# Norm, turn and router of the first layer norm done one token tile at a time, in a kernel of two transformer blocks

## The chip, the cores and the metric

The program runs on one core of one Trainium2 chip. The metric is the device time in microseconds (us) of one execution. Before the change three executions took 1676.92 to 1677.72 us, median 1677.66 us.

## The reference

The input x has 256 tokens of 1024 numbers (two tiles of 128 tokens, t = 0 and 1). It passes through a first block of two layers (retention and stick-breaking attention, then SwiGLU), and then through a second block of two layers, l = 0 and 1. All is float32. One layer of the second block, cut to what matters here:

```python
mix = hybrid_mixer(x, ...)                       # three kinds of attention, then a product with w_o
x = layer_norm(ALPHA * x + mix, ln1_g, ln1_b)    # "the first norm"
# hier_moe:
lg = x @ rg_w + rg_b                             # 4 groups; the best group per token
le = x @ re_w + re_b                             # 8 experts a group; the best two of that group
y = sum over experts of gate * (silu(x @ w_gate) * (x @ w_up)) @ w_down
x = layer_norm(ALPHA * x + y, ln2_g, ln2_b)
```

## The kernel before

The program is written engine by engine, each with its own instruction stream, and semaphores join them. An engine executes strictly in the order of its stream. A helper `Signal` numbers the increments of a semaphore by layer, so that `x.at(l, k)` is the k-th increment in layer l.

**Products.** Dense weights are 1 MB units that SyncE's queue loads into a ring of six slots. ScalarE (ACT, L917 and L933) writes the rounded high half of a unit, VectorE (DVE, L924 and L939) the low half, and TensorE (PE) does three products of halves for each full one (L946, L947, L950).

**Dummies.** `keep_running(acc, n)` (L1256) issues n matmuls of 512 columns on ones whose result nobody reads. They are there so that TensorE is not idle.

**The stretch that is changed, once per layer of the second block.** `output_unit(3)` finishes the four quarters `wo` of the attention output (two halves of columns for each token tile). VectorE adds each to H (L2887) and takes its moments (L2877, L2898, L2899). GpSimd (POOL) takes the power -1/2 (L3239), one number per token. VectorE then computes `shift` for tile 0 (L2892). ScalarE writes the normed tile 0, Z[:, 0] (L2262), and VectorE tile 1 (L2902). Both read H with a stride of 8 elements and write Z in blocks, so that each block of 128 columns holds every eighth column of H. TensorE, after 16 dummies, turns (transposes) the sixteen 128x128 blocks (`turn_z`, L1580); a bank `xT2` holds two values of k for both tiles. ScalarE and VectorE take four k each out of the banks to T8, with gain and bias of the norm (L2268, L2906). The router (L1788) multiplies T8 with 36 columns: eight k times two tiles, in the order in which the k come. Next to that ScalarE writes H_high, the rounded high half of Z (L2259), and VectorE H_low, the rest (L2882), in both tiles with the low half of tile 1 placed after `chosen` and ahead of `rank`.

**From the router to the experts.** VectorE runs a chain of small operations on the logits (L2916 to L2942, ending in `chosen_done`). TensorE meanwhile issues 8 and 4 dummies, and then counts ranks (L1799 to L1803). VectorE makes rank (L2962) and the first one-hot picks (L2953, `make_picks(0, 0)`), then goes on to the gate weights (L2965 to L2988, `gate_done`), with two small exponentials on ScalarE in between. TensorE gathers the tokens of the first two pairs of experts ("duos") by matmuls with the picks (`gather(0, f)`, L1819): for each of four banks, two k, and for each k high and low half of both tiles, 32 in all. It waits for both low halves before. `turn_picks(0)` (L1833) waits for `gate_done`. ScalarE (L2284) and VectorE (L3002) take the gathered banks to XG; `gate_up2(0)` (L1860) starts the experts.

**The experts.** Sixteen duos follow one another on TensorE; per duo the weights are 6 MB. SyncE's queue issues a load when the slot it goes to is released by TensorE. One slot of duo 0 lies in T8, and is loaded once the router is filled.

**The seam between the blocks.** After the last product of the first block TensorE issues 26 dummies, then `turn_stream` turns both tiles of H (L1568). For layer 1 five dummies lie between its tiles, for layer 0 none. Tile t is ready after `last_norm(t)` (VectorE, L2630). ScalarE splits three weight units (L933) and then the turned stream (L2160), from which the first projection is fed.

Of the kernel before, what the change touches and what calls it, by code (L numbers as in the profile page):

```python
# [345 lines left out]
def build(nc, src, out, debug=None):  # L346
# [7 lines left out]
    with ctx:  # L354
# [311 lines left out]
        head_var = signal("head_var", HR)  # L666
# [29 lines left out]
        xT2_act = signal("xT2_act", 4)  # L696
# [51 lines left out]
        split_high = signal("split_high", TT)  # L748
# [18 lines left out]
        def in_blocks(view):  # L767
            return view.rearrange("p (k n) -> p k n", k=KT)

# [36 lines left out]
        for kp in range(4):  # L806
            read2["xT", kp] = (bT_low, kp + 5)
            read2["xT2", kp] = ((xT2_act, xT2_dve)[kp % 2], 2 * (kp // 2) + 2)
# [426 lines left out]
        def _(pe):  # L1235
# [324 lines left out]
            def turn_stream(l):  # L1560

                for t in range(TT):
# [8 lines left out]
                    if t == 0 and l > 0:  # L1571
                        keep_running(bank2(("A", 1)), 5)

            def turn_z(l):

                for t, done in enumerate((z_act, z_dve)):
                    pe.wait_ge(done.sem, done.at(l, 1))
                    for k in range(KT):
                        acc = claim2(("xT2", k // 2), l) if t == 0 and k % 2 == 0 else bank2(("xT2", k // 2))
                        mm = nc.tensor.transpose(acc[:, k % 2 * SEQ + t * P:k % 2 * SEQ + (t + 1) * P],  # L1580
                                                 Z[:, t, k * P:(k + 1) * P], ident[:])
                        if t == TT - 1 and k % 2 == 1:
                            fill(mm, ("xT2", k // 2))
# [120 lines left out]
            keep_running(bank_of(("gu", 2 * PAIRS - 1)), 26)  # L1704
            for l in range(LAYERS):
# [75 lines left out]
                keep_running(bank2(("xT2", 3)), 16)  # L1781
                turn_z(l)
                acc = bank2(("router", 0))
                for n, k in enumerate((0, 2, 1, 3, 4, 6, 5, 7)):
                    signal_ = (xT2_act, xT2_dve)[k // 2 % 2]
                    pe.wait_ge(signal_.sem, signal_.at(l, k // 4 * 2 + k % 2 + 1))
                    for t in range(TT):
                        mm = nc.tensor.matmul(acc[:, t * 64:t * 64 + 36], T8[:, k, t * P:(t + 1) * P], rw[:, k, :],  # L1788
                                              start=(n == 0 and t == 0), stop=(n == KT - 1 and t == TT - 1))
# [15 lines left out]
                def moe_pass(pass_):  # L1805
# [5 lines left out]
                    def gather(g, n):  # L1811
# [4 lines left out]
                        for j, k in enumerate((2 * n, 2 * n + 1) if group_parts(g) == 4 else (n,)):  # L1816
                            for n_ in range(2 * TT):
                                t, part = divmod(n_, 2)
# [5 lines left out]
                                                      start=(n_ == 0), stop=(n_ == 2 * TT - 1))  # L1824
                        fill_p(mm, "xg", g, n)
# [157 lines left out]
        def _(act):  # L1983
# [179 lines left out]
            for l in range(LAYERS):  # L2163
# [93 lines left out]
                def high_of_z(t):  # L2257

                    nc.scalar.activation(moe_split(H_high[:, t, :]), Z[:, t, :], ACT.Copy).then_inc(split_high.sem, 1)  # L2259
# [1013 lines left out]
```

## Time and profile before

| what | us |
|---|---|
| three executions, median | 1677.66 |
| the profiled execution, its own time | 1679.14 |
| its span, first to last instruction | 1677.4 |
| TensorE busy | 1645.6 (98%) |
| VectorE busy | 856.5 (51%) |
| ScalarE busy | 651.1 (39%) |
| GpSimd busy | 172.1 (10%) |

The mean granted clock of TensorE is 0.995 of full speed. Busy TensorE counts dummies too, so 98% does not say that the engine does useful work all the time. In the second block of layer 0 the stretch of the change is at 1007 to 1030 us of the span, in layer 1 at 1415 to 1438 us. The seam between the blocks is at 855 to 863 us. The rows below give start, duration and what ended the idle time before.

### The profile page before, as it was taken

How to read it: one execution, taken by the hardware profiler on the slowest of the kernel's cores; microseconds unless marked ns; L12 is line 12 of the kernel's file. 1: busy time of each engine (PE TensorE's matmuls, PEld its weight loads, DVE VectorE, ACT ScalarE, POOL GpSimd, SP SyncE). 2: the span in 40 equal slices, each digit the busy share in tenths (PEclk: the TensorE clock that was granted, in tenths of full speed). 3: DMA queues.
4: the chain of work that ended last, by engine and by line, in shares of the span. 5: the costliest groups of instructions: out<-in, count | busy, mean ns of one | idle time of the engine just before them, and what ended most of it. 6: DMA issues, size and time to landing. Idle time of an engine off the chain costs nothing. (4 is left out here: it accounts for less than half of the span.)

```text
span 1677.4 us, 23534 instructions
## 1 busy us (share of the span) xinstructions
PE 1645.6 (98%) x9403; PEld 1244.0 (74%) x9403; DVE 856.5 (51%) x1420; ACT 651.1 (39%) x920; POOL 172.1 (10%) x242
## 2 busy tenths in 40 slices
PE   9999999999999999999999999999999999999997
PEld 7888879999798887999988975444448887544442
DVE  6566564444646556544456867322126785532223
ACT  5455444343445454434345453111114464211111
POOL 2020001111202000111111040000002023000000
PEclk9999999999999999999999999999999999999999
DMA  8544545553654455455356546999995636699996
GB/s 319 180 146 147 179 151 183 194 178 123 235 184 134 151 176 176 167 185 188 137 185 194 189 142 231 408 421 421 421 397 191 192 127 241 228 421 420 421 417 259
DMA packets 158587, 396.61 MB, mean 236 GB/s; under 512 B 20752, under 2 KB 85264, under 8 KB 140048
## 3 DMA queue, kind: packets, MB, share of 16 engines
q1 hardware_dynamic: 158480, 395.18, 64.6%
q8 instruction: 67, 1.10, 0.3%
q14 instruction: 40, 0.33, 0.1%
HBM read 394.10 MB, written 1.05 MB: 236 GB/s over the span
## 5 line engine op out<-in xcount | busy, mean ns | idle before, releaser
L946 PE MATMUL ps<-split,split 128*128 128x256 f32 (+3 forms) x1872 | 631.6, 337 | 1.2 <-DVE split L939 0.7
L950 PE MATMUL ps<-split,split 128*128 128x256 f32 (+3 forms) x1872 | 627.6, 335 | 0.1
L947 PE MATMUL ps<-split,split 128*128 128x256 f32 (+3 forms) x1872 | 623.6, 333 | 0.0
L924 DVE TENSOR_TENSOR split<-ring,split 128x2048 fp32r<-128x2048 f32 x136 | 312.5, 2305 | 253.9 <-ACT split L917 253.8
L946 PEld LDWEIGHTS ps<-split,split 128*128 128x128 f32 x1872 | 351.6, 188 | 36.1 <-issue 2.1
L950 PEld LDWEIGHTS ps<-split,split 128*128 128x128 f32 x1872 | 351.7, 188 | 35.8 <-DVE split L2389 1.2
L947 PEld LDWEIGHTS ps<-split,split 128*128 128x128 f32 x1872 | 352.9, 189 | 33.0 <-issue 0.5
L917 ACT ACTIVATE split<-ring 128x2048 fp32r<-128x2048 f32 x136 | 260.3, 1916 | 278.1 <-PE ps L950 268.7
L1860 PE MATMUL ps<-ring,arena 128*64 128x512 f32 x464 | 105.7, 592 | 0.0
L3040 DVE SCALAR_TENSOR_TENSOR arena<-arena,ps 128x256 f32<-128x256 f32 x32 | 15.4, 480 | 169.8 <-ACT arena L2306 134.1
L1860 PE MATMUL ps<-arena 128*64 128x512 f32 x288 | 99.5, 594 | 0.5 <-SPq L1208 0.5
L939 DVE TENSOR_TENSOR split<-ring,split 128x1536 fp32r<-128x1536 f32 (+3 forms) x44 | 80.8, 1852 | 25.2 <-ACT split L933 25.0
L1860 PE MATMUL ps<-high,arena 128*64 128x512 f32 x256 | 92.0, 592 | 1.6 <-DMA arena<-in_expert_w_up 1.6
L3052 DVE TENSOR_TENSOR split<-ps,split 128x512 fp32r<-128x512 f32 x64 | 44.3, 692 | 92.2 <-ACT split L2313 92.2
L2306 ACT ACTIVATE arena<-ps 128x256 f32<-128x256 f32 x32 | 12.3, 384 | 202.9 <-PE ps L1860 202.9
L933 ACT ACTIVATE split<-ring 128x1536 fp32r<-128x1536 f32 (+3 forms) x44 | 67.7, 1547 | 49.2 <-PE ps L950 48.4
L1860 PEld LDWEIGHTS ps<-ring,arena 128*64 128x64 f32 x464 | 34.3, 137 | 64.0 <-issue 63.9
L2313 ACT ACTIVATE split<-ps 128x512 fp32r<-128x512 f32 x64 | 38.2, 597 | 107.1 <-PE ps L1886 107.1
L1860 PEld LDWEIGHTS ps<-high,arena 128*64 128x64 f32 x256 | 29.1, 137 | 60.2 <-issue 60.2
L1900 PE MATMUL ps<-split,split 128*128 128x512 f32 x240 | 64.2, 402 | 0.0
L1819 PEld LDWEIGHTS ps<-split,split 128*128 128x128 f32 x320 | 43.9, 190 | 25.2 <-issue 25.2
L1886 PE MATMUL ps<-ring,arena 128*64 128x512 f32 x256 | 58.5, 598 | 0.1
(260 smaller groups left out, 1698.8 us busy)
## 6 DMA issues: line engine op xcount, KB each, us to landing
ring<-in_w_in SPq DMA_DIRECT2D x52, 1024.0 KB, 5.1
ring<-in_w_gate_up SPq DMA_DIRECT2D x44, 1024.0 KB, 5.3
ring<-in_expert_w_down SPq DMA_DIRECT2D x32, 1024.0 KB, 13.0
ring<-in_w_down SPq DMA_DIRECT2D x22, 1024.0 KB, 4.9
ring<-in_w_in SPq DMA_DIRECT2D x28, 768.0 KB, 4.5
ring<-in_expert_w_gate SPq DMA_DIRECT2D x20, 1024.0 KB, 11.8
ring<-in_expert_w_up SPq DMA_DIRECT2D x20, 1024.0 KB, 13.8
arena<-in_expert_w_down SPq DMA_DIRECT2D x16, 1024.0 KB, 14.5
```

The source lines that it names most:

```text
L917: nc.scalar.activation(split(high[:, n % HIGH, :]), ring[:, units[key], :], ACT.Copy).then_inc(high_done.sem, 1)
L924: nc.vector.tensor_tensor(split(slot), slot, split(high[:, n % HIGH, :]), ALU.subtract).then_inc(low_done.sem, 1)
L933: nc.scalar.activation(split(high[:, n % HIGH, 0:used(key)]), ring[:, units2[key], 0:used(key)], ACT.Copy).then_inc(high2_done.sem, 1)
L939: nc.vector.tensor_tensor(split(slot), slot, split(high[:, n % HIGH, 0:used(split2[n])]), ALU.subtract).then_inc(low2_done.sem, 1)
L946: nc.tensor.matmul(acc, sh, mh, start=start, stop=False)
L947: nc.tensor.matmul(acc, *second, start=False, stop=False)
L950: return nc.tensor.matmul(acc, *third, start=False, stop=stop)
L1819: mm = nc.tensor.matmul(acc[:, j * SEQ:j * SEQ + XG_cols[g]].rearrange("p (e n) -> p e n", n=TAKEN_SLOTS), moe_split((H_high, H_low)[part] ...
L1860: mm = nc.tensor.matmul(acc[i * SLOTS:(i + 1) * SLOTS, :].rearrange("p (s n) -> p s n", s=2), XG[g % 2][:, at:at + SLOTS], w_[:, :, k % w_ ...
L1886: mm = nc.tensor.matmul(bank2(("yg", 0, d, half))[i * SLOTS:(i + 1) * SLOTS, :], hT[:, d % 2, j * P + i * SLOTS:j * P + (i + 1) * SLOTS], ...
L1900: mm = nc.tensor.matmul(bank2(("sc", 0, i)), moe_split(pickT[:, d % 2, (TT - 1 - t) * P:(TT - t) * P]), moe_split(Y[:, part, half * 512:(h ...
L3052: nc.vector.tensor_tensor(moe_split(Y[:, 1, cols]), acc, moe_split(Y[:, 0, cols]), ALU.subtract).then_inc(y_low.sem, 1)
```

## The change

Tile 0 and tile 1 are handled one after the other. Z is written in the columns' own order; whoever needs blocks reads it with a stride. The 16 dummies before the turns become 6, the 26 at the seam become 10, and five more stand between the tiles of the stream in layer 0 as well. ScalarE takes all eight k of tile 0 and four of tile 1 to T8, VectorE four of tile 1, in instructions of half the size. The high half of tile 0 is made by GpSimd, that of tile 1 by ScalarE at the end; both low halves remain on VectorE, that of tile 0 ahead of the logits, that of tile 1 after the first picks. `shift` moves to GpSimd. The first gather does the high halves of all four banks first and then the low halves.

```diff
-            keep_running(bank_of(("gu", 2 * PAIRS - 1)), 26)
+            keep_running(bank_of(("gu", 2 * PAIRS - 1)), 10)
...
-                    if t == 0 and l > 0:
+                    if t == 0:
                         keep_running(bank2(("A", 1)), 5)
...
+            def turn_z(t, l):
+                done = (z_act, z_dve)[t]
+                pe.wait_ge(done.sem, done.at(l, 1))
+                for k in range(KT):
+                    key = ("xT2", 2 * t + k // 4)
+                    acc = claim2(key, l) if k % 4 == 0 else bank2(key)
+                    mm = nc.tensor.transpose(acc[:, k % 4 * P:(k % 4 + 1) * P], Z[:, t, k::KT], ident[:])
+                    if k % 4 == 3:
+                        fill(mm, key)
+            def route(t, l):
+                acc = bank2(("router", 0))
+                ks = range(KT) if t == 0 else (0, 4, 1, 5, 2, 6, 3, 7)
+                for n, k in enumerate(ks):
...
+                    mm = nc.tensor.matmul(acc[:, t * 64:t * 64 + 36], T8[:, k, t * P:(t + 1) * P], rw[:, k, :],
+                                          start=(n == 0 and t == 0), stop=(n == KT - 1 and t == TT - 1))
...
-                keep_running(bank2(("xT2", 3)), 16)
-                turn_z(l)
...
+                keep_running(bank2(("xT2", 3)), 6)
+                turn_z(0, l)
+                route(0, l)
+                turn_z(1, l)
+                mm = route(1, l)
                 fill(mm, ("router", 0))
...
-                        pe.wait_ge(split_low.sem, split_low.at(l, TT))
+                        pe.wait_ge(split_high.sem, split_high.at(l, 1))
+                        pe.wait_ge(high1_in.sem, high1_in.at(l, 1))
...
-                    for f in range(group_parts(0)):
-                        gather(0, f)
+                    for part in range(2):
+                        if first and part == 1:
+                            pe.wait_ge(split_low.sem, split_low.at(l, TT))
+                        for f in range(group_parts(0)):
+                            gather(0, f, part)
... ScalarE
-                nc.scalar.activation(in_blocks(Z[:, 0, :]), H[:, 0, :].rearrange("p (n k) -> p k n", k=KT), ACT.Identity,
-                                     scale=rstd2[:, 0:1], bias=shift[:, 0:1]).then_inc(z_act.sem, 1)
-                act.wait_ge(z_act.sem, z_act.at(l, 1))
-                high_of_z(0)
-                for k in (0, 1, 4, 5):
+                nc.scalar.activation(Z[:, 0, :], H[:, 0, :], ACT.Identity, scale=rstd2[:, 0:1],
+                                     bias=shift[:, 0:1]).then_inc(z_act.sem, 1)
+                for t, k in [(0, k) for k in range(KT)] + [(1, k) for k in range(4, KT)]:
...
                 act.wait_ge(z_dve.sem, z_dve.at(l, 1))
-                high_of_z(1)
+                nc.scalar.activation(moe_split(in_blocks(H_high[:, 1, :])), of_blocks(Z[:, 1, :]),
+                                     ACT.Copy).then_inc(high1_in.sem, 1)
... VectorE
-                    if i == 3:
-                        dve.wait_ge(rstd_done.sem, rstd_done.at(l, 1))
-                        nc.vector.scalar_tensor_tensor(out=shift, in0=mv2[:, 0, 0:1], scalar=-1.0, in1=rstd2[:, 0:1], ...)
...
-                nc.vector.tensor_scalar(in_blocks(Z[:, 1, :]), H[:, 1, :].rearrange("p (n k) -> p k n", k=KT), ...)
-                for k in (2, 3, 6, 7):
+                nc.vector.tensor_scalar(Z[:, 1, :], H[:, 1, :], mv2[:, 1, 0:1], rstd2[:, 1:2], ALU.subtract, ALU.mult)
+                for k in range(4):
...
-                low_of_z(0)
+                dve.wait_ge(split_high.sem, split_high.at(l, 1))
+                nc.vector.tensor_tensor(moe_split(in_blocks(H_low[:, 0, :])), of_blocks(Z[:, 0, :]), ...)
...
-                low_of_z(1)
                 dve.wait_ge(chosen_done.sem, chosen_done.at(l, 1))
...
                 make_picks(0, 0)
+                dve.wait_ge(high1_in.sem, high1_in.at(l, 1))
+                nc.vector.tensor_tensor(moe_split(in_blocks(H_low[:, 1, :])), of_blocks(Z[:, 1, :]), ...)
... in the expert loop, duos 1 and 3: the same product of Z and gain, now without rearranging
-                                out=H[:, d // 2, :].rearrange("p (n k) -> p n k", k=KT),
-                                in0=Z[:, d // 2, :].rearrange("p (k n) -> p n k", k=KT), scalar=ALPHA,
+                                out=H[:, d // 2, :], in0=Z[:, d // 2, :], scalar=ALPHA, in1=lng[:, 0, :], op0=ALU.mult,
... GpSimd, after the power of tile 0
+                        nc.gpsimd.tensor_scalar(shift, mv2[:, 0, 0:1], rstd2[:, 0:1], -1.0, ALU.mult,
+                                                ALU.mult).then_inc(shift_in.sem, 1)
+                wait_apart(pool, z_act.sem, z_act.at(l, 1))
+                wait_apart(pool, z_dve.sem, z_dve.at(l, 1))
+                nc.gpsimd.tensor_copy(moe_split(in_blocks(H_high[:, 0, :])),
+                                      of_blocks(Z[:, 0, :])).then_inc(split_high.sem, 1)
```

## Rows read from the trace of the kernel before

**Rows 1.** Timeline of TensorE, layer 0 (start us, us, engine line operation count)

```profile
1011.26 3.63 PE L1259 MATMUL ps<-ones 128*128 128x512 bf16 x16
1014.82 1.97 PE L1580 MATMUL ps<-ident,arena 128*128 128x128 f32 x16
1016.79 3.76 PE L1788 MATMUL ps<-arena,T 128*128 128x36 f32 x32
1020.38 2.76 PE L1259 MATMUL ps<-ones 128*128 128x512 bf16 x12
...
1025.85 3.77 PE L1819 MATMUL ps<-split,split 128*128 128x160 f32 x32 [0.99 <-DVE split L2953]
1029.46 0.40 PE L1833 MATMUL ps<-split 128*128 128x192 f32 x2
```

**Rows 2.** Timeline of ScalarE, layer 0

```profile
1012.53 2.24 ACT L2262 ACTIVATE arena<-H,arena 128x1024 f32<-128x1024 f32 x1 [9.25 <-DVE arena L2892]
...
1016.17 1.93 ACT L2268 ACTIVATE T<-ps,arena 128x256 f32<-128x256 f32 x4 [0.30 <-PE ps L1580]
...
1028.77 0.86 ACT L2284 ACTIVATE arena<-ps,arena 128x160 f32<-128x160 f32 x2 [0.93 <-PE ps L1819]
```

**Rows 3.** Timeline of VectorE, layer 0

```profile
1016.39 1.90 DVE L2906 TENSOR_SCALAR T<-ps,arena 128x256 f32<-128x256 f32 x4 [0.79 <-PE ps L1580]
...
1020.66 0.23 DVE L2916 TENSOR_TENSOR arena<-ps,arena 128x72 f32<-128x72 f32 x1 [1.10 <-PE ps L1788]
...
1023.55 1.22 DVE L2882 TENSOR_TENSOR split<-arena,split 128x1024 fp32r<-128x1024 f32 x1
1024.69 0.22 DVE L2962 SCALAR_TENSOR_TENSOR arena<-ps,arena 128x64 f32<-128x64 f32 x1
1024.94 0.76 DVE L2953 SCALAR_TENSOR_TENSOR split<-arena 128x256 fp32r<-128x256 f32 x2
...
1028.13 0.23 DVE L2988 TENSOR_TENSOR split<-arena,split 128x64 fp32r<-128x64 f32 x1
1028.28 0.79 DVE L3002 TENSOR_SCALAR arena<-ps,arena 128x160 f32<-128x160 f32 x2
```

**Rows 4.** Timeline of GpSimd, layer 0

```profile
1010.70 0.57 POOL L3239 TENSOR_TENSOR arena<-arena,minus_half 128x1 f32<-128x1 f32 x1 [21.75 <-DVE arena L2899]
```

**Rows 5.** Groups by line and shape, whole span (count, busy us, mean ns, idle before)

```profile
L2341 ACT ACTIVATE arena<-H,arena 128x1024 f32<-128x1024 f32 x4 | 4.6, 1150 | 5.7 <-DVE arena L3083 5.7
L3174 POOL CAST split<-arena 128x256 fp32r<-128x256 f32 x44 | 17.5, 397 | 305.3 <-DVE arena L2604 303.9 <-issue 1.4
L3243 POOL TENSOR_SCALAR arena<-arena 128x1 f32<-128x1 f32 x4 | 0.8, 190 | 490.2 <-ACT arena L2341 490.0
```

**Rows 6.** Timeline of TensorE, layer 1, the same stretch

```profile
1424.54 4.29 PE L1788 MATMUL ps<-arena,T 128*128 128x36 f32 x32
1428.63 3.93 PE L1259 MATMUL ps<-ones 128*128 128x512 bf16 x12
```

**Rows 7.** Stretches: span, busy us (count) of PE, PEld, DVE, ACT, POOL; granted clock, DMA share, GB/s

```profile
1428.00:1429.00 1.00, 1.00 (x5) 0.77 (x6) 0.07 (x1) 0.00 (x0) 0.00 (x0) 0.50 1.06 438
1028.00:1036.00 8.00, 8.00 (x47) 3.89 (x48) 7.29 (x25) 2.14 (x3) 0.00 (x0) 1.00 0.03 10
1048.00:1250.00 202.00, 200.82 (x968) 92.76 (x965) 47.92 (x102) 35.12 (x70) 0.00 (x0) 1.00 1.01 416
```

**Rows 8.** Timelines at the seam between the blocks: TensorE, ScalarE, VectorE

```profile
855.08 5.79 PE L1259 MATMUL ps<-ones 128*128 128x512 bf16 x26
860.70 1.96 PE L1568 MATMUL ps<-ident,H 128*128 128x128 f32 x16
...
859.72 1.59 ACT L933 ACTIVATE split<-ring 128x1664 fp32r<-128x1664 f32 x1 [0.83 <-DMA ring<-in_w_in]
862.01 2.38 ACT L2160 ACTIVATE split<-ps 128x256 fp32r<-128x256 f32 x8 [0.70 <-PE ps L1568]
...
858.02 1.28 DVE L2630 SCALAR_TENSOR_TENSOR H<-H,stat,arena 128x1024 f32<-128x1024 f32 x1 [0.66 <-POOL stat L3137]
```

More of the change, by code:

```diff
@@ L665, in build @@
         gates = signal("gates", 4)
-        head_var = signal("head_var", HR)
+        head_var = signal("head_var_then_high1", HR)
         head_rstd = signal("head_rstd", HR)
@@ L695, in build @@
         bT_low = signal("bT_low", 16)
-        xT2_act = signal("xT2_act", 4)
+        xT2_act = signal("xT2_act", 12)
         xT2_dve = signal("xT2_dve", 4)
@@ L746, in build @@
         resid_in = signal("resid_in", 2 * TT)
-        split_high = signal("split_high", TT)
+        split_high = signal("split_high", 1)
+        high1_in = Signal(head_var.sem, 1, LAYERS * HR)
         split_low = signal("split_low", TT)
@@ L768, in in_blocks, with of_blocks @@
             return view.rearrange("p (k n) -> p k n", k=KT)
+        def of_blocks(view):
+            return view.rearrange("p (n k) -> p k n", k=KT)
         def bank_of(key):
@@ L1570, in turn_stream @@
                             fill(mm, ("xT", b))
-                    if t == 0 and l > 0:
+                    if t == 0:
                         keep_running(bank2(("A", 1)), 5)
[L1574 to L1583, printed above, removed]
+            def turn_z(t, l):
[11 more added lines that the diff above has]
+                for n, k in enumerate(ks):
+                    if t == 0:
+                        pe.wait_ge(xT2_act.sem, xT2_act.at(l, k + 1))
+                    elif k < 4:
+                        pe.wait_ge(xT2_dve.sem, xT2_dve.at(l, k + 1))
+                    else:
+                        pe.wait_ge(xT2_act.sem, xT2_act.at(l, 8 + k - 3))
+                    mm = nc.tensor.matmul(acc[:, t * 64:t * 64 + 36], T8[:, k, t * P:(t + 1) * P], rw[:, k, :],
+                                          start=(n == 0 and t == 0), stop=(n == KT - 1 and t == TT - 1))
+                return mm
             def index_scores(h, l):
@@ L1780, in _ @@
                 output_unit(3, l)
-                keep_running(bank2(("xT2", 3)), 16)
-                turn_z(l)
[L1783 to L1789, printed above, removed]
+                keep_running(bank2(("xT2", 3)), 6)
[3 more added lines that the diff above has]
+                mm = route(1, l)
                 fill(mm, ("router", 0))
@@ L1809, in fill_p, with gather @@
                         mm.then_inc(filled[banks2[(name, 0) + key]], 1)
-                    def gather(g, n):
+                    def gather(g, n, only=None):
                         lo, hi = GROUP_DUOS[g]
@@ L1817, in gather @@
                             for n_ in range(2 * TT):
-                                t, part = divmod(n_, 2)
+                                part, t = divmod(n_, TT)
+                                if only not in (None, part):
+                                    continue
                                 mm = nc.tensor.matmul(acc[:, j * SEQ:j * SEQ + XG_cols[g]].rearrange(
@@ L1823, in gather @@
                                                           "p (e n) -> p e n", n=SLOTS)[:, :, 0:TAKEN_SLOTS]),
-                                                      start=(n_ == 0), stop=(n_ == 2 * TT - 1))
-                        fill_p(mm, "xg", g, n)
+                                                      start=(n_ == 0 and (j == 0 or only is None)),
+                                                      stop=(n_ == 2 * TT - 1 and (only is None or j == 1)))
+                        if only != 0:
+                            fill_p(mm, "xg", g, n)
                     def turn_picks(d):
@@ L2889, in _ @@
                                                    op1=ALU.add).then_inc(wo_in.sem, 1)
-                    if i == 3:
-                        dve.wait_ge(rstd_done.sem, rstd_done.at(l, 1))
-                        nc.vector.scalar_tensor_tensor(out=shift, in0=mv2[:, 0, 0:1], scalar=-1.0, in1=rstd2[:, 0:1],
-                                                       op0=ALU.mult, op1=ALU.mult).then_inc(shift_in.sem, 1)
                     dve.wait_ge(wo_in.sem, wo_in.at(l, i + 1))
@@ L2964, in _ @@
                 make_picks(0, 0)
+                dve.wait_ge(high1_in.sem, high1_in.at(l, 1))
+                nc.vector.tensor_tensor(moe_split(in_blocks(H_low[:, 1, :])), of_blocks(Z[:, 1, :]),
+                                        moe_split(in_blocks(H_high[:, 1, :])), ALU.subtract).then_inc(split_low.sem, 1)
                 nc.vector.tensor_tensor(shifted, logit[:, :, 0:GROUPS],
```

25 lines of the change are left out of this document (11 added, 14 removed).

## The prediction

> **What bounds the kernel now.** I read the view of stretches first, for the places where something other than the products ends the wait. Expert weights fill the DMA engines from 1048 to 1250 us (share 1.01), but from 1028 to 1036 us they stand nearly still (0.03) [rows 7]. So the stream of weights has no backlog when the experts begin, and its later loads go out as TensorE releases slots: what TensorE gains ahead of the experts moves the stream too, and comes out at the end. Then the timelines of the engines over the stretch of the norm. TensorE looks busy, but from 1011.26 to 1014.8 and again from 1020.38 it is busy with dummies [rows 1]; the work is a chain over engines. ScalarE waits 9.25 us for `shift` and then needs 2.24 us for Z [rows 2]; the turns start 0.05 us behind its end, at 1014.82; the router's passes run one behind another for 3.76 us, each pair a matmul of float32 in two passes, so 3.76 / 32 = 0.118 us a pass, twice that a product [rows 1]. VectorE starts on the logits at 1020.66, and at 1023.55, right behind the chain's end, it puts 1.22 us of low half in front of rank, which starts at 1024.69 [rows 3]. The gather starts at 1025.85, `turn_picks` at 1029.46 [rows 1], and the experts 0.3 us later. All this is on the path, twice in the program. At the seam of the blocks the turns stand behind 26 dummies until 860.70, while tile 1 was ready at 858.02 + 1.28 = 859.30 [rows 8].
>
> **The seam.** A dummy takes 3.63 / 16, less the tail of the last, about 0.22 us [rows 1]. Ten end at 855.08 + 2.2 = 857.3, the turns of tile 0 (half of 1.96) at 858.2, five dummies at 859.3, the turns of tile 1 at about 860.3, 2.2 us before now. ScalarE is the next to be late: its third weight unit ends at 859.72 + 1.59 = 861.31, bound by that unit's landing, which the change does not touch. So L2160 starts at 861.3 instead of 862.01 [rows 8], and **0.7 us** of the 2.2 remain. Bounds: 0 (if VectorE's low halves of the next unit are what counts) and 2.2.
>
> **Z of tile 0.** The power ends at 1010.70 + 0.57 = 1011.27 [rows 4]; a POOL operation on one number takes 0.19 us [rows 5], with the hand-over some 0.4, so `shift` is there at 1011.7 instead of about 1012.5. The stride goes from the read: the nearest row without one is 1.15 us [rows 5] instead of 2.24. Z is ready at 1012.85 instead of 1014.77. Six dummies end at 1011.26 + 1.3 = 1012.6, so they do not hold it. Tile 1's Z on VectorE is not late even at today's speed, since today all turns are done at 1016.8.
>
> **Turns and router.** Eight turns take half of 1.97. The first bank is full 0.6 us after the start, 1013.45. ScalarE takes now eight small pieces: four of 256 columns take 1.93 us, two of 160 take 0.86 [rows 2], so 0.46 and 0.4 us a piece; I take 0.36 for 128 columns (bounds 0.25, half the row of 256 with its pipeline, and 0.46). Eight end at 1013.5 + 8 x 0.36 = 1016.4. TensorE's router for tile 0 goes at their pace and ends 0.4 later; being in order, the turns of tile 1 are behind it: 1016.85 to 1017.8. Then VectorE's four pieces from 1017.5 (1.90 us for 256 columns today [rows 3], 1.3 to 1.4 for 128) to 1018.9, ScalarE's four from 1017.95 to 1019.45, and the last product ends at about 1020.0. Router for router: 1020.5 now, so 0.5 us. At 0.25 us a piece it would be 1.8 us, at 0.46 a loss of 0.7.
>
> **Halves.** VectorE has the low half of tile 0 behind its pieces: 1018.9 + 1.22 = 1020.1. It is as late as the router, so logits start at 1020.2 instead of 1020.66: **0.45 us**. The low half waits for GpSimd's copy. A cast of 256 columns takes 0.397 us [rows 5], 1024 some 1.5 us; it starts behind both Z, at 1015.6 at the latest, and has until 1018.9. No row shows GpSimd reading with this stride; ScalarE with it needed 2.24 for 1.15, and twice 1.5 still ends at 1018.6. It costs nothing up to 3.3 us. The Trainium skill (GPSIMD Engine Reference, Performance pitfalls for Q7 kernels) gives +50% for reads with a step over 8 bytes; by that it would end near 1017.9, an estimate from that page. ScalarE's high half of tile 1, at most 2.24 us from 1019.5, is there before 1022. The 1.22 us between `chosen` and rank go: the ranks' matmuls take some 0.4 us in their place, so rank starts 0.45 + 0.65 = **1.1 us** earlier, and so does the gather: 1024.75.
>
> **Gather.** Its 16 high products (1.9 us) cover the low half of tile 1, which now follows the picks on VectorE and ends at 1025.8. Hidden; without that cover it would cost 1.0 us. But VectorE's chain to `gate_done` begins behind it. That chain takes from 1025.70 to 1028.36 now [rows 3]; behind 1025.7 it ends at 1028.4, no earlier. TensorE ends its gather at 1024.75 + 3.6 = 1028.35. `turn_picks` starts at 1028.45 instead of 1029.46: **1.0 us** for layer 0. The banks now fill only in the second half of the gather, but still 0.47 us apart; ScalarE has its first at 1028.2 and VectorE at 1029.1, before `gate_up2` asks at 1028.8 and 1029.6. The slot in T8 is asked for only at its second half, 3.5 us on, when the weights, still from 1028 on, have landed. The straight product in duos 1 and 3 shortens VectorE under TensorE's cover: nothing.
>
> **The clock.** In layer 1 the granted clock was 0.50 from 1428 to 1429 us, the lower level of 1.2 GHz [rows 7], after the turns and most of the router. In layer 0 the same router products kept their pace of 2.4 GHz. The router took 4.29 instead of 3.76 us, the twelve dummies 3.93 instead of 2.76 [rows 1, 6]. Without a fall after the change, layer 1 gains 1.0 and these 0.5: **1.5 us**. But the change takes ten full dummies away, and spreads the same thin products over 7.4 us (1012.6 to 1020.0), with gaps, where it was 5.6. I expect the fall more often. Its price: at the least the 0.53 of the router and, of the dummies' 1.17 us, what exceeds their slack (they end 0.65 us before `chosen`), 0.5: 1.05 us. At the most the tile 1 turns and all router products of tile 1 run at half rate: turns 0.9 longer, the products 16 x 0.118 = 1.9 longer less what waits on ScalarE anyhow: 2.5 us. I take 1.8. The Trainium skill (TensorE: Matmul & The Clock Gate, Avoid-throughput-drops row of Why this matters for your kernels) warns of gaps between bursts of matmuls, which speaks against this change; this trace agrees as far as that the clock fell behind thin work, while the engine was busy throughout.
>
> **The sum.** Without a fall 0.7 + 1.0 + 1.5 = 3.2 us less; the profiled execution of 1679.14 (span 1677.4, 1.7 around it) would be 1675.9. It was 1.5 above the median of the runs, 1677.66, which would be 1674.5. With one fall 1.8 goes: 1676.3.
>
> **Rivals.** *No fall:* 1674.5. For it: layer 0 had none. Chance 0.25. *Deep falls in both layers*, the case on the other side: 2.5 us in each, so 3.2 - 5.0, 1.8 us slower, 1679.5. It decides from 1.6 us a layer on. For it: the thinner sequence and the fall in layer 1. Against it: the late fall there cost only 0.5 us. Chance 0.2. *The weights hide it:* if the stream from 1048 on is the bound whatever TensorE does before, only the seam counts: 1677.0. Against it the still DMA from 1028 to 1036. Chance 0.05. *Smaller pieces cost as much as large ones:* 0.46 us a piece, 12 on ScalarE in a row, takes 1.2 a layer away from my 1.0 and 1.5: 1674.5 + 2.4 = 1676.9 without a fall, 1679.0 with two at the least price. Chance 0.1.
>
> **Numbers.** The forecast, one fall of middle price or two cheap ones, has 0.4: 1676.3 us, its own range 1675 to 1677.7. From the cheap end of the pieces without a fall to deep falls it is 1673.6 to 1679.7, which I give as range. 0.2% is 3.4 us, about what a measurement here can tell from no change: faster than 1674.3 takes the case without a fall and pieces a little cheaper than mine, or a fall in layer 1 before that is usual and now gone: 0.29. Slower than 1681.0 takes deep falls and dear pieces: 0.06. The rest, 0.65, is within.
>
> **What would show it.** After: Z of tile 0 at 1.1 to 1.2 us in ScalarE's rows, turns right behind; pieces of 128 columns at 0.36 us; logits about 0.45 us earlier after the last w_o product than now and rank 0.4 us behind `chosen`; gather without idle between its halves; granted clock of 0.5 in at least one layer between turns and ranks; L2160 0.7 us earlier at the seam. I would be wrong if VectorE waits for GpSimd at the low half of tile 0, if idle time stands before `gate_up2(0)`, or if TensorE's idle time behind the weights (DMA) grows by what the front gained.

## The result, and the profile after

The changed kernel takes 1682.7 us, the median of 8 executions (1681.63 to 1683.89), the kernel before in the same session 1677.69 us (8 executions, 1676.71 to 1678.17). The ratio is 1.003, 95% interval 1.0021 to 1.0039: slower by 5.0 us. The forecast was 1676.3 us, with a range up to 1679.7. The profiled execution took 1681.64 us, its span 1679.9. Of all executions below, one, at 3856.43 us (e10), is a disturbed one and counts in no ratio.

The first view is TensorE's timeline in layer 0, with ScalarE, VectorE and GpSimd behind it (start us, us, engine line operation, count, idle time and its releaser).

```profile
1010.61 1.47 PE L1263 MATMUL ps<-ones 128*128 128x512 bf16 x6
1012.41 1.16 PE L1585 MATMUL ps<-ident,arena 128*128 128x128 f32 x8 [0.33 <-ACT arena L2281]
...
1016.36 1.12 PE L1585 MATMUL ps<-ident,arena 128*128 128x128 f32 x8
1017.54 2.24 PE L1600 MATMUL ps<-arena,T 128*128 128x36 f32 x16
...
1025.14 3.97 PE L1836 MATMUL ps<-split,split 128*128 128x160 f32 x32 [0.40 <-DVE split L2963]
1029.75 0.47 PE L1852 MATMUL ps<-split 128*128 128x192 f32 x2 [0.64 <-DVE split L3001]
...
1011.12 1.24 ACT L2281 ACTIVATE arena<-H,arena 128x1024 f32<-128x1024 f32 x1 [8.48 <-POOL arena L3254]
1013.16 2.90 ACT L2285 ACTIVATE T<-ps,arena 128x128 f32<-128x128 f32 x8 [0.81 <-PE ps L1585]
...
1018.90 2.08 ACT L2289 ACTIVATE split<-arena 128x1024 fp32r<-128x1024 f32 x1
...
1017.08 1.36 DVE L2915 TENSOR_SCALAR T<-ps,arena 128x128 f32<-128x128 f32 x4 [2.56 <-PE ps L1585]
1018.36 2.01 DVE L2918 TENSOR_TENSOR split<-arena,split 128x1024 fp32r<-128x1024 f32 x1
...
1020.53 0.23 DVE L2927 TENSOR_TENSOR arena<-ps,arena 128x72 f32<-128x72 f32 x1
...
1024.91 2.13 DVE L2976 TENSOR_TENSOR split<-arena,split 128x1024 fp32r<-128x1024 f32 x1
...
1029.47 0.23 DVE L3001 TENSOR_TENSOR split<-arena,split 128x64 fp32r<-128x64 f32 x1
...
1014.69 2.03 POOL L3258 CAST split<-arena 128x1024 fp32r<-128x1024 f32 x1 [1.02 <-DVE arena L2911]
```

The starts of two profiles differ by what happened long before, so times are counted here from the end of the last product of w_o, where the first dummies begin (1011.26 before [rows 1], 1010.61 after). Turns start at 1.80 (3.56 before), and the last router product ends at 9.17 (9.29). But the logits start on VectorE at 9.92, later than before (9.40), with no idle time in front: the engine had only just ended its low half (L2918), which takes 2.01 us now that it reads Z with a stride, where L2882 took 1.22 [rows 3]. (Its other two operands, the high half that it reads and the low half that it writes, lie in blocks and are gone through straight, before and after: one operand of three has the stride.) The second low half (L2976) takes 2.13, pushes the gate weights (L3001) back, and the gather takes 3.97 us where it took 3.77 [rows 1]; `turn_picks` (L1852) then stands idle 0.64 us for the gate weights. Before there was no idle time there [rows 1]; it started at 18.20, now at 19.14.

In layer 1 more is lost. TensorE's timeline, and then the view of stretches (span, busy us and count of PE, PEld, DVE, ACT, POOL, granted clock, DMA share, GB/s):

```profile
1421.05 3.06 PE L1600 MATMUL ps<-arena,T 128*128 128x36 f32 x16
1423.91 1.95 PE L1585 MATMUL ps<-ident,arena 128*128 128x128 f32 x8
...
1426.41 3.20 PE L1600 MATMUL ps<-arena,T 128*128 128x36 f32 x14 [0.26 <-ACT T L2285]
1429.42 4.92 PE L1263 MATMUL ps<-ones 128*128 128x512 bf16 x12
...
1440.36 0.47 PE L1852 MATMUL ps<-split 128*128 128x192 f32 x2 [0.65 <-DVE split L3001]
```

```profile
1422.00:1423.00 1.00, 1.00 (x8) 0.84 (x7) 0.00 (x0) 1.00 (x5) 0.94 (x1) 1.00 1.01 373
1423.00:1424.00 1.00, 1.00 (x7) 0.90 (x7) 0.00 (x0) 0.44 (x2) 1.00 (x1) 0.78 1.05 442
1424.00:1425.00 1.00, 1.00 (x6) 1.00 (x6) 0.00 (x0) 0.00 (x0) 0.09 (x1) 0.50 0.99 418
...
1432.00:1433.00 1.00, 1.00 (x4) 0.42 (x3) 0.66 (x6) 0.00 (x0) 0.00 (x0) 0.50 0.95 348
1433.00:1434.00 1.00, 1.00 (x5) 0.34 (x3) 0.00 (x0) 0.00 (x0) 0.00 (x0) 0.60 0.92 340
```

The granted clock was at 0.50, the lower level of 1.2 GHz, from about 1423.6 to 1433.8 us: 10 us. The profile of before had 3.4 us of it, from about 1427.6 to 1431.0 [rows 7]; the stretches at its two ends:

```profile
1427.00:1428.00 1.00, 1.00 (x10) 1.00 (x9) 0.30 (x6) 0.00 (x0) 0.00 (x0) 0.80 0.99 414
...
1430.00:1431.00 1.00, 1.00 (x4) 0.35 (x3) 0.88 (x5) 0.00 (x0) 0.00 (x0) 0.50 0.96 369
```

The eight turns of tile 1 take 1.95 us instead of 1.12 and the twelve dummies 4.92 [rows 6: 3.93]. The experts start 22.79 us after w_o, before 19.06.

The seam, TensorE and ScalarE:

```profile
855.23 2.33 PE L1263 MATMUL ps<-ones 128*128 128x512 bf16 x10
857.50 1.16 PE L1572 MATMUL ps<-ident,H 128*128 128x128 f32 x8
...
859.58 1.10 PE L1572 MATMUL ps<-ident,H 128*128 128x128 f32 x8
...
859.93 1.59 ACT L937 ACTIVATE split<-ring 128x1664 fp32r<-128x1664 f32 x1 [0.89 <-DMA ring<-in_w_in]
861.42 2.37 ACT L2183 ACTIVATE split<-ps 128x256 fp32r<-128x256 f32 x8
```

ScalarE's eight pieces follow the weight unit without idle time. From the dummies' start they begin at 6.19 us, before at 6.93 [rows 8].

The clock is on record for every execution as a mean over the span. The kernel before had 0.9956 on average in 21 executions (0.993 to 0.998); the changed one 0.992 or 0.993 in all of its 8. If the clock is either whole or half, a mean c has 2(1-c) of the span at the lower level: 15 us before, 25 us after. Not all of this costs time: from 1670 us to the end, where TensorE has no work left, both profiles stand at 0.50 to 0.52, 7.4 us of it before and some 10 after. What counts is ahead of that: before, 6.8 us at the turns of layer 1's stream (1264 to 1270 us) and the 3.4; after, 3.4 us at the same turns (1267 to 1270) and the 10. The mean still goes with the time: of 71 executions of the kernel before in three sessions, those at 0.998 took 1675.0 to 1677.4 us, those at 0.993 1679.0 to 1680.8.

### The profile page after: what moved, and what is told of

Its sections match the earlier page's. It is cut to its first block and busy times, and to the rows that moved or that the text cites. A ratio compares the mean times of both kernels' runs of the same rounds, so it can differ in the third digit from the quotient of the medians.

```text
span 1679.9 us, 23498 instructions
## 1 busy us (share of the span) xinstructions
PE 1645.4 (98%) x9372; PEld 1245.0 (74%) x9372; DVE 855.1 (51%) x1418; ACT 654.0 (39%) x934; POOL 177.0 (11%) x246
## 3 DMA queue, kind: packets, MB, share of 16 engines
HBM read 394.10 MB, written 1.05 MB: 235 GB/s over the span
```

## Experiments

Medians are of 5 to 11 executions, beside the kernel before in the same session (its medians there: 1677.95, 1677.57 and 1677.92); the ratio with its 95% interval decides. This table has the steps of the profiles (those of e1 and e3 apart), in us after the last product of w_o, layer 0 / layer 1:

```
kernel              router ends    turn_picks     first gate_up   mean clock of its executions
before               9.29 /  9.82  18.20 / 18.73  18.53 / 19.06   0.993 to 0.998
after                9.17 / 11.64  19.14 / 22.39  19.53 / 22.79   0.992 to 0.993
eight fills (e2)     9.33 /  9.32  19.33 / 19.31  19.73 / 19.71   0.995 to 0.997
straight+fills (e5)  9.31 /  9.31  17.73 / 17.73  18.13 / 18.13   0.996 to 0.998
Z in blocks (e6)    10.25 / 10.25  18.66 / 18.67  19.06 / 19.07   0.996 to 0.997
before, six (e9)     9.27 / 10.68  18.18 / 19.96  18.51 / 20.28   0.991 to 0.995
after, sixteen (e11)11.65 / 12.88  22.69 / 23.98  23.08 / 24.37   0.991 to 0.997
order alone (e7)     9.28 /  9.29  17.70 / 17.72  18.10 / 18.12   0.996 to 0.998
seam alone (e4)      9.29 /  9.29  18.21 / 18.20  18.54 / 18.53   0.995 to 0.998
low half later (e8)  9.29 /  9.29  18.57 / 17.62  18.90 / 17.95   0.994 to 0.998
e8, 24 dummies (e10) 9.79 /  9.29  18.56 / 17.61  18.89 / 17.94   0.996 to 0.998
```

**e1: the halves straight.** My theory was the stride of the halves, the rival the clock.

```diff
-                nc.vector.tensor_tensor(moe_split(in_blocks(H_low[:, 0, :])), of_blocks(Z[:, 0, :]),
-                                        moe_split(in_blocks(H_high[:, 0, :])), ALU.subtract).then_inc(split_low.sem, 1)
+                nc.vector.tensor_tensor(moe_split(H_low[:, 0, :]), Z[:, 0, :],
+                                        moe_split(H_high[:, 0, :]), ALU.subtract).then_inc(split_low.sem, 1)
...              # the low half of tile 1 and both high halves likewise; in the gather
-                                                      moe_split((H_high, H_low)[part][:, t, k * P:(k + 1) * P]),
+                                                      moe_split((H_high, H_low)[part][:, t, k::KT]),
```

> The changed kernel, but H_high and H_low keep the columns' own order, so that the four casts and low halves read and write without a stride, and TensorE's gathers take their weights with the stride instead (k::8). Theory 'stride' (the two strided low halves of 2.0 and 2.1 us on VectorE make gate_done late, and turn_picks waits for it): low halves back to 1.2 us, turn_picks no longer waits for L3001, 1.3 us a layer, together 2.6: about 1680.1 us. Theory 'clock' (falls of the granted clock around the router hold most of the loss): no change, 1682.7 us. If strided weight loads cost TensorE something, the gather's 3.97 us grow and the time is above 1682.7.

1713.43 us, ratio 1.0214 (1.02 to 1.0228): neither theory's time. Its timeline, VectorE and then TensorE (PEld is its weight load):

```profile
1018.37 1.22 DVE L2918 TENSOR_TENSOR split<-arena,split 128x1024 fp32r<-128x1024 f32 x1
...
1026.51 1.22 DVE L2976 TENSOR_TENSOR split<-arena,split 128x1024 fp32r<-128x1024 f32 x1
1026.71 7.75 PEld L1836 LDWEIGHTS ps<-split,split 128*128 128x128 f32 x32 [0.87 <-issue]
1026.74 7.93 PE L1836 MATMUL ps<-split,split 128*128 128x160 f32 x32 [0.40 <-DVE split L2963]
```

The low halves are back at 1.22 us, so the stride in the read of Z is what made them 2.01 and 2.13 (the text of the expectation calls it a stride in what is read and written; only the read of Z had it). But the 32 gather products with strided weights take 7.93 us, not 3.97. Over the program the gathers keep TensorE busy for 91.1 us instead of 55.4, which is more than the whole loss of 30.7 against the changed kernel. The stride was moved to where it costs most; the expectation named this case, without a price.

**e3: e1 with the fills of e2** (the next experiment) repeats it.

> Both edits together. If stride and clock add up: 2.6 and 3 us, about 1677 us, or below. If only one of them holds, the same as the better of the two alone.

1708.81 us, ratio 1.0183 (1.0169 to 1.0196), not the 1677 hoped for: the strided gathers are in it too. It is 4.6 less than e1, with 17 us of the lower level between w_o and the first experts' products of the two layers where e1 has 27, which goes with the clock.

**e2: full dummies among the thin products.** Only the clock is to change.

```diff
     turn_z(0, l)
+    keep_running(bank2(("ranks", 0)), 2)
     route(0, l)
     turn_z(1, l)
+    keep_running(bank2(("ranks", 0)), 2)
...  # in route: behind every second product of tile 0
+    if t == 0 and n % 2 == 1:
+        keep_running(bank2(("ranks", 0)), 1)
```

> The changed kernel with eight dummies a layer more, put where TensorE waits for pieces anyway: two behind the turns of tile 0, one behind every second product of the router for tile 0, two behind the turns of tile 1. Theory 'clock': the granted clock stays at 1.0 in both layers, the spread of the executions (1681.6 to 1683.9) shrinks, and 2 to 4 us go: about 1679.5 us. Theory 'stride': 1682.5 to 1683 us, since the low halves stay.

1679.22 us (11 executions), ratio 1.0006 (0.9997 to 1.0015): 3.5 us less than the changed kernel, as the clock theory said. The spread did not shrink, though (1676.9 to 1680.93). In the view of stretches its layer 1 has no fall between w_o and the experts:

```profile
1422.00:1426.00 4.00, 4.00 (x31) 3.61 (x31) 1.29 (x3) 2.40 (x8) 2.03 (x1) 1.00 1.03 419
1426.00:1430.00 4.00, 3.83 (x26) 2.51 (x24) 3.79 (x15) 3.31 (x5) 0.00 (x0) 1.00 1.00 415
1430.00:1434.00 4.00, 2.73 (x18) 1.31 (x19) 3.30 (x16) 0.00 (x0) 0.00 (x0) 1.00 0.88 349
```

Both layers are alike now, and `turn_picks` at 19.33 is 1.1 later than in layer 0 before: what the strides cost is left, less what the new order gains.

**e5: straight halves, contiguous gather weights, fills.** A measurement of the halves' stride by itself. The edit is that of e2 and, for the halves, that of e1; the gather stays as in the changed kernel. Its weights keep their blocks, so the rearranging of the columns is left out and the gather takes other columns than it should.

> The changed kernel with the eight fill dummies, and with the casts and low halves going straight through (no stride on either side), while the gathers take contiguous blocks as before. What the gathers bring together is then the wrong columns: the rearranging is left out of the computation, the work is the same in number and size. Theory 'stride': low halves 1.2 us instead of 2.0 and 2.1, logits 0.5 us earlier, gate_done 1.4 us earlier, turn_picks at the gather's end; 1.2 to 1.3 us a layer less than with the fill dummies alone (1679.2): about 1676.7 us. Rival 'tile order' (the small pieces and the late filled banks hold turn_picks): no more than 0.3 a layer, 1678.6 us.

1676.77 us, ratio 0.9991 (0.9982 to 1.0), 2.45 below e2 (2.07, if each is taken against the kernel before of its own session). Its rows, GpSimd, VectorE, TensorE:

```profile
1015.60 1.04 POOL L3262 CAST split<-arena 128x1024 fp32r<-128x1024 f32 x1 [1.02 <-DVE arena L2915]
...
1019.41 1.21 DVE L2922 TENSOR_TENSOR split<-arena,split 128x1024 fp32r<-128x1024 f32 x1
1020.94 0.23 DVE L2931 TENSOR_TENSOR arena<-ps,arena 128x72 f32<-128x72 f32 x1 [0.18 <-PE ps L1600]
...
1029.25 0.47 PE L1856 MATMUL ps<-split 128*128 128x192 f32 x2
```

Now the logits wait for the router, 0.18 us, as I had forecast for the changed kernel, and `turn_picks` has no idle time. It stands 1.6 us earlier than in e2 in each layer. That 3.2 us of steps became 2.1 to 2.45 in the medians. But the logits start at 9.42, no earlier than in the kernel before (9.40), and `turn_picks` has gained 0.47 on it, not 1.0: the strides are not all that the forecast had wrong.

**e6: Z in blocks again, halves straight.** The version of this that gathers the right columns.

```diff
-  nc.scalar.activation(Z[:, 0, :], H[:, 0, :], ...)            # tile 1 on VectorE likewise
+  nc.scalar.activation(in_blocks(Z[:, 0, :]), of_blocks(H[:, 0, :]), ...)
-  transpose(..., Z[:, t, k::KT], ident[:])
+  transpose(..., Z[:, t, k * P:(k + 1) * P], ident[:])
...              # the fills as in e2, the halves as in e1
```

> The changed kernel with the fill dummies and Z written in blocks as in the kernel before, so that only the two norms have the stride (2.24 us on ScalarE, 1.24 on VectorE) and halves and turns are contiguous; tile order, dealing of the halves and gather order stay. Stride: the turns of tile 0 start 1.0 us later, but the low halves are short: turn_picks 0.7 us earlier than with the fill dummies alone, about 1677.7 us. If the tile order itself costs, it stays at 1679 us or goes above.

1677.55 us, ratio 1.0001 (0.9992 to 1.001). The router ends 0.92 us later than in e2, which is the stride in Z, and `turn_picks` still 0.67 earlier. A stride in the norm ahead of the turns (ScalarE's Z of tile 0, 2.23 us for 1.24) costs the path less than one in the two low halves behind them.

**e4: the seam alone**, on the kernel before.

```diff
-            keep_running(bank_of(("gu", 2 * PAIRS - 1)), 26)
+            keep_running(bank_of(("gu", 2 * PAIRS - 1)), 10)
-                    if t == 0 and l > 0:
+                    if t == 0:
```

> The kernel before with only the change at the seam of the blocks (10 dummies for 26, five between the tiles in layer 0 too). All theories: 0.65 us less, 1677.0 us. If it is above the kernel before, the seam has a cost that the timelines do not show (a lower clock behind it).

1675.8 us, ratio 0.9989 (0.998 to 0.9998). The first projection starts 6.82 us after the dummies' start, before 7.46. The time is down by 2.15 in the medians, by 0.3 to 3.4 us by the interval, which holds the forecast 0.7.

**e9: the kernel before with six dummies instead of sixteen ahead of the turns.** Nothing else changed.

```diff
-                keep_running(bank2(("xT2", 3)), 16)
+                keep_running(bank2(("xT2", 3)), 6)
```

> The kernel before with 6 dummies instead of 16 ahead of the turns, nothing else. Theory 'clock': TensorE now stands idle 2.2 us ahead of the turns, and the granted clock falls in the router in more executions; 1 to 3 us slower than the kernel before, 1679.5 us, executions spread wider. Rival (the fall comes from the thin products of tile 0 at the pace of the pieces, not from missing dummies): 1677.9 us, no change.

1682.55 us, ratio 1.0029 (1.0018 to 1.0041). Ten dummies that nobody reads, 2.2 us of them, behind which the turns waited 0.05 us at most, are worth some 5 us (3 to 7 by the interval), more than the 1 to 3 of the expectation; the spread (1678.46 to 1683.22) is no wider than before. Stretches of its layer 1:

```profile
1420.00:1422.00 2.00, 1.78 (x10) 1.78 (x11) 1.00 (x1) 1.23 (x2) 0.00 (x0) 0.65 1.01 412
1422.00:1424.00 2.00, 2.00 (x12) 2.00 (x10) 1.25 (x3) 1.68 (x4) 0.00 (x0) 0.50 1.01 426
1424.00:1426.00 2.00, 2.00 (x20) 2.00 (x19) 1.90 (x8) 1.20 (x2) 0.00 (x0) 0.99 1.00 410
1426.00:1428.00 2.00, 2.00 (x15) 1.53 (x15) 0.48 (x3) 0.00 (x0) 0.00 (x0) 0.86 1.00 414
1428.00:1430.00 2.00, 2.00 (x6) 0.71 (x5) 1.73 (x13) 0.00 (x0) 0.00 (x0) 0.50 0.90 313
```

Two falls in one layer. In this profile they cost 1.8 us against its own layer 0 (20.28 for 18.51), 1.2 more than the fall in the profile of before (19.06). This execution was the fastest of its seven, at 1678.46 us and a mean clock of 0.995; the other six had 0.991 to 0.993 and took 1680.51 us or more. The profile shows that falls come, the medians what they cost; I have no profile of an execution at the median.

**e11: the changed kernel with sixteen dummies.** If the missing dummies were the whole cause, this would bring the clock back.

```diff
-                keep_running(bank2(("xT2", 3)), 6)
+                keep_running(bank2(("xT2", 3)), 16)
```

> The changed kernel with one edit taken back: 16 dummies instead of 6 ahead of the turns. Clock theory: of the changed kernel's loss of some 5 us the strided halves make 1.0 a layer and the rest is the granted clock; with sixteen dummies no fall to 0.50 lies between the turns and the ranks of layer 1, but the turns start behind the dummies, about 1.7 us later than in the changed kernel (2.2 us of dummies less the wait that they cover), of which the thin chain behind passes on all: the experts' first product comes some 1.5 us later after the last product of w_o than in layer 0 of the changed kernel (19.5), at 21.0, in both layers. 1677.7 - 0.7 + 2 x (21.0 - 18.5) = about 1682, no better than the changed kernel (1682.7), with both layers alike. Rival (the thin order of turns and router lets the clock fall whatever stands ahead): the fall in layer 1 stays at 8 to 10 us, layer 1 another 3 us later than layer 0, 1685 or more.

1685.12 us, ratio 1.0039 (1.0025 to 1.0052). The executions lie far apart, 1681.16 to 1688.09 us. The profiled one, the slowest, has falls in both layers:

```profile
1020.00:1022.00 2.00, 2.00 (x12) 2.00 (x12) 2.00 (x6) 2.00 (x3) 0.00 (x0) 0.54 1.01 418
1022.00:1024.00 2.00, 2.00 (x7) 0.77 (x7) 1.48 (x10) 0.53 (x1) 0.00 (x0) 0.50 0.75 264
...
1430.00:1432.00 2.00, 1.75 (x10) 1.55 (x8) 1.45 (x5) 0.60 (x2) 0.00 (x0) 0.50 1.01 420
...
1436.00:1438.00 2.00, 2.00 (x6) 0.71 (x5) 1.73 (x13) 0.00 (x0) 0.00 (x0) 0.50 0.90 254
```

The clock theory as I put it for this run is refuted: the falls are there with sixteen dummies too, some 10 us in layer 1 and 7 in layer 0, and four of the five executions have a mean clock of 0.991 to 0.994. The fifth, 0.997 and 1681.16 us, is where that theory had put the kernel without a fall (about 1682). The rival (the thin order lets the clock fall whatever stands ahead) had the place and the 1685 right; layer 1 is only 1.3 us behind layer 0, not 3, because layer 0 falls too. With e2 and e9: fewer dummies let the clock fall in the old order, the new order lets it fall in most executions even with all of them, and eight dummies spread in the new order keep it up (0.995 to 0.997 in all 11 executions of e2). What e11 can't tell apart is the order and the delay: its dummies also push the turns back, to 3.46 us after w_o.

**e7: the order alone.** The kernel before with the seam, the low half of tile 1 behind the first picks, and the gather's high halves first; halves and Z as before.

```diff
                 last.then_inc(chosen_done.sem, 1)
-                low_of_z(1)
...
                 make_picks(0, 0)
+                low_of_z(1)
...              # and the gather in two parts, as in the changed kernel
```

> The kernel before with the seam of the change, the low half of tile 1 behind the first picks and the first gather with the high halves first; no tile order, no stride moved. Rank starts 0.6 us earlier than before, but the chain to gate_done runs behind the low half: turn_picks 0.45 us earlier a layer. With the seam's 1675.8 that gives 1674.9 us. If gather order costs something that I don't see, 1675.8 or more.

1676.3 us, ratio 0.9992 (0.9983 to 1.0001), expected 1674.9. Its timeline, VectorE and TensorE:

```profile
1026.23 1.22 DVE L2889 TENSOR_TENSOR split<-arena,split 128x1024 fp32r<-128x1024 f32 x1
1026.46 3.77 PE L1821 MATMUL ps<-split,split 128*128 128x160 f32 x32 [0.40 <-DVE split L2959]
1030.16 0.47 PE L1837 MATMUL ps<-split 128*128 128x192 f32 x2
```

The gather covers the low half without idle time in it, and `turn_picks` comes at 17.70 and 17.72, 0.5 us earlier than in layer 0 before (18.20). Beside e4 (1675.8) the 1.0 us of the two layers can't be seen in the median.

**e8: the low half behind `below`**, so that ScalarE's exponentials run beside it.

```diff
-                make_picks(0, 0)
-                low_of_z(1)
+                make_picks(0, 0)
...              # behind the instruction that ends below_done
+                low_of_z(1)
```

> Kernel before with the seam of the changed one, and the low half of tile 1 behind `below` instead of right behind the first picks: the exponentials of ScalarE then run beside the low half. Theory (VectorE's chain to `gate_done` is what `turn_picks` waits for, and in the version with the low half right behind the picks ScalarE's exponentials begin behind `shifted`, 1.2 us late): `turn_picks` starts 0.1 to 0.3 us earlier a layer than there (17.70 after the last product of w_o), 1676.0. Rival (the chain of VectorE is a plain sum of its instructions, so their order does not matter): 17.70 again and 1676.3.

1676.56 us, ratio 0.9991 (0.9982 to 1.0). In layer 1 `turn_picks` is at 17.62, 0.1 earlier than in e7, and the first `gate_up` at 17.95, 0.17 earlier; e10 repeats both (17.61 and 17.94). That is the bottom of what the theory gave, small but the same twice; the medians can't show it. Layer 0 had a fall of the clock in both profiles and can't be compared.

**e10: e8 and 24 instead of 14 dummies after layer 0's experts.**

```diff
-                            keep_running(bank2(("yg", 0, 0, 0)), 14)
+                            keep_running(bank2(("yg", 0, 0, 0)), 24)
```

> The kernel with the low half of tile 1 behind `below`, and 24 instead of 14 dummies after layer 0's experts, ahead of the combination. Theory (the fall of the granted clock to 0.50 at 1263 to 1270 us, at the turns of layer 1's stream, comes after idle time of TensorE ahead of it, and costs up to 2 us): no fall there and 1 to 2 us less than the kernel with 14, 1674.5. Rival (the ten more dummies stand ahead of the combination, and the fall comes from the stretch behind it): the fall stays, and the time is the same or up to 2.2 us longer, 1676 to 1678.

1676.34 us, ratio 0.9991 (0.9982 to 1.0). Stretches at layer 1's stream turns (from 1267.51 us in e8, from 1265.09 in e10), e8 and then e10:

```profile
1267.00:1271.00 4.00, 3.49 (x13) 2.31 (x14) 2.20 (x2) 0.01 (x1) 0.00 (x0) 0.59 0.11 19
```

```profile
1263.00:1267.00 4.00, 1.91 (x13) 1.43 (x14) 2.44 (x2) 0.26 (x1) 0.00 (x0) 1.00 0.09 10
1267.00:1271.00 4.00, 4.00 (x30) 3.74 (x29) 2.93 (x9) 2.39 (x8) 0.00 (x0) 1.00 0.02 4
```

The fall is gone from the profile, as the theory said, but the 1 to 2 us did not come. The two profiles say why: counted from the first of these dummies, the turns start at 7.60 us instead of 6.26, and from there to the first projection it is 3.02 instead of 4.68. The clock gives back 1.66 and the ten dummies take 1.34. Whether that holds in every execution stays open. No version's median is below the kernel before by more than 0.13%; the seam alone is as good as any.

## Why the prediction was wrong

**What it had right.** *The seam*: 0.7 us forecast, 0.74 in the profile, and ScalarE is what is late next. *Z of tile 0*: forecast 1.15 us and turns 1.6 us after w_o, measured 1.24 and 1.80. *Pieces of 128 columns*: 0.36 us (eight in 2.90). *The cover of the gather* over the low half of tile 1 (e7). *GpSimd's copy* ended at 1016.72, before VectorE asked at 1018.4, though the stride nearly doubled it (2.03 us, 1.04 straight in e1: +95%, where the prediction quotes the Trainium skill, GPSIMD Engine Reference, Performance pitfalls for Q7 kernels, with +50%; the measurement decides). *What the front gains or loses comes out at the end*: behind the start of layer 1's experts eleven profiles (before, after, e2, e4 to e11) all take 239.1 to 239.8 us. Small misses among these, 0.2 for the later turns and 0.2 for the last product, left 0.12 us of the router's 0.5: its last product ends at 9.17, not at the forecast 8.74.

**The step that failed: "VectorE has the low half of tile 0 behind its pieces: 1018.9 + 1.22 = 1020.1".** I took 1.22 us from a row in which every operand lay straight [rows 3], for an instruction that the change makes read one of its operands, Z, with a stride of 8 elements. It took 2.01, and the one of tile 1 2.13. For ScalarE I had doubled the price [rows 2: 2.24 for 1.15], and for GpSimd too; for VectorE, whose two instructions are the ones on the path, I had not. From that follow both misses behind it. The logits start at 9.92 instead of the forecast 8.94 after w_o: along VectorE 0.79 of this is the stride and 0.2 the late pieces. And in "behind 1025.7 it ends at 1028.4, no earlier", the gate weights end at 19.09 instead of 17.14: 0.98 from the logits, 0.91 from the second low half. So `turn_picks` has lost 0.94 us where I had it gain 1.0. Over two layers that is 2 us against the kernel before, and 4 us against the forecast. e5 shows it from the other side: without the strides `turn_picks` is 0.47 us ahead of before, and 1.6 ahead of e2. It also shows a second, smaller failure, "the last product ends at about 1020.0" (8.74 after w_o): with straight halves the router, at 9.31, holds the logits to 9.42, and half of the forecast 1.0 us a layer is still missing. So of the 1.95 us a layer that the forecast was off, some 1.4 (19.14 for e5's 17.73) go with the strides, and some 0.5 stay without them.

The Trainium skill has the rule that I passed over (SBUF — State Buffer, Door 1: The DMA port swizzle): consecutive accesses within one 16-byte line are at full bandwidth, each that crosses to a new line pays. Here a step is 32 bytes, and the trace agrees: 1.22 to 2.01 and 2.13 on VectorE. Another page of the Trainium skill (VectorE: DVE Perf Modes, Mode 1× (REGULAR) — the baseline) says that this mode "makes no assumptions" and that float32 with "weird strides" works in it. That is no price: it does work here, but not at the same speed.

**The term that was mis-sized: the clock.** I gave one fall of 1.8 us, at most 2.5, and set 0.4 on it. The mechanism was the one named (ten full dummies away, the same thin products spread over a longer time), but in all 8 executions the mean clock was 0.992 or 0.993. In the profiled one (0.993) layer 1 reached the gather 3.23 us later than its own layer 0, and the median difference to e2 is 3.5. My upper bound had counted turns and products of tile 1, but not the twelve dummies behind them: the level stayed low through all of them, 4.92 us where eight and four had taken 2.93, and VectorE's chain no longer covered that. I had also called the sixteen dummies' removal free apart from this risk; e9 shows a loss of about 5 us by itself. By the rival of deep falls in both layers I had 1679.5. The profile has one deep fall, in layer 1, and none in layer 0; that one alone cost more (3.2) than I had given to a deep fall (2.5), and the rival too was built on strides at no price.

**The sum.** Seam -0.74, layers' fronts +2.0 (0.94 to 1.0 each), clock +3.5 by e2: +4.7, measured +5.0 (3.5 to 6.5 by the interval). The first two are from profiles and the last from medians, and e2's own dummies put `turn_picks` 0.2 us back a layer, so the agreement within 0.3 is luck in part. The pair of profiles alone gives less, 2.5 us between the spans: -0.65 up to layer 0's last w_o product, +1.00 and +3.73 in the two fronts, -1.39 from layer 0's experts to layer 1's w_o, and -0.19 behind layer 1's experts. The -1.39 belongs to the pair and not to the change: that middle part takes 387.1 to 389.8 us in the eleven profiles, and the profile of before, with 6.8 us of the lower level at the stream's turns, is near the top. Where in the span the falls of the other seven executions of the changed kernel were has no profile and stays open.

## What to carry to other kernels

Price every operand that changes its layout on every engine that reads it, and first on the one that sets the path; a duration from a row holds only for the same strides. Taking a stride from one reader gives it to the next: the best place is the one that runs least often, or has cover. A dummy that hides nothing in the profile may still hold the clock up; take dummies away in an experiment of their own, over enough executions, before building on their time.

## What the runs showed of the hardware

- **A stride of 8 elements (32 bytes) in one operand that is read, 1024 columns of float32, the result written straight.** VectorE, two operands read, one of them with the stride: 1.22 us becomes 2.01 to 2.16. VectorE with one read: 0.81 becomes 1.22 to 1.25. ScalarE: the copy 1.06 becomes 2.08, the norm 1.24 becomes 2.24. GpSimd's cast: 1.04 becomes 2.03. None of these writes had a stride, so what a strided write costs stays open.
- **TensorE's weights with that stride.** 32 loads of rounded halves take 7.75 instead of 3.85 us, and the products behind them 7.93 instead of 3.97 (e1; 3.77 where the low half of tile 1 is short, e5 to e7). Transposes of float32 that read Z with the same stride take nearly what straight ones do at the same place: tiles 0 and 1 in 1.16 and 1.05 us (e2), straight in 1.09 and 1.04 (e6).
- **Clock.** Removing ten of sixteen dummies cost about 5 us with no other change; the ten back in the new order did not help (1685.12), eight spread among its products did (1679.22). The level fell while TensorE was busy with transposes and products of 36 columns, and stayed low through the twelve full dummies behind (4.92 us for 2.93).
